# Rotary embedding without a swapped copy of its input, and half a chunk of weights made later

## The chip, the cores and the metric

One core of a Trainium2 chip runs the whole program. The metric is the device time of one execution in microseconds (us). Engines: TensorE (PE) multiplies matrices, with its weight loads shown apart as PEld; VectorE (DVE) and ScalarE (ACT) do elementwise work; GpSimd (POOL) does nothing here but set a tile to one; SyncE (SP) issues the DMAs.

## What is computed

Two transformer blocks on 256 tokens of 1024 features, float32. The first has a mixer with two kinds of attention, MLA (8 heads, 64 plain and 32 rotated query and key features) and a forgetting attention ("fox"), and a gated feed-forward with a convolution over three tokens. The second has two layers (differential attention, then MOBA), each with a squared-ReLU feed-forward. What the change touches is the rotation:

```
def rope(x, positions):
    ...
    x1, x2 = xf[..., : r // 2], xf[..., r // 2:]
    out = jnp.concatenate([x1 * cos - x2 * sin, x2 * cos + x1 * sin], axis=-1)

q = ((q_lat normed) @ w_uq).reshape(b, s, MLA_HEADS, 96)   # 64 plain, 32 to be rotated
k_mla = concatenate([k_nope, broadcast(k_rope, 8 heads)])
scores = q_mla . k_mla * MLA_SCALE                          # contracted over 96 features
```

## The kernel before, in words

**Weights.** All weights but the adaptive ones (ada) are read once, in chunks of 128 partitions by 2048 columns (`weight_order`, chunk n is `ORDER[n]`). A chunk goes by DMA into one of four raw buffers, then in two halves of 1024 columns into whi (rounded to the short float32 form; ScalarE, line 1545, for three chunks VectorE, line 1941) and wlo (the remainder, VectorE, line 1949). TensorE forms each product in three matmuls, whi by high part, whi by low part, wlo by high part (lines 1070 to 1072). whi and wlo have three slots, four from chunk ("out", 0) on. The step `weights` of chunk n + 3 (or n + 4) is put where chunk n is done, by `refill(n)`, and waits for chunk n's last matmul in the slot that it takes. `refill` also takes one of the waiting small jobs (`chores`).

**Order.** `stages()` writes one list of steps; each engine's program walks through the list and issues its own part of every step. So an engine's queue has the order of the list, and an instruction waits behind all that stands ahead of it.

**The rotary part.** ("uq", 0) holds the 512 plain query features, ("uq", 1) the 512 others: for each of 8 heads the 32 rotary features, and again the same 32 with their halves swapped. Each is three weight tiles deep (384 latent features), 1536 columns used. ("uq", 1) runs in two pairs of banks, `pr` 0 (rotary) and 1 (swapped): 2 x 2 x 3 x 3 = 36 matmuls. In step `ev_uq_rope` VectorE multiplies the first by COS and the second by SIN (line 2219), whose sign was set per partition by the step `signs` (line 2055), and adds both, 512 columns (line 2223). In `copy_rope` ScalarE copies the result in four instructions to rows 64 to 96 of QM (line 1719). The key's 32 rotary features are treated alike: `turn_key` (lines 2208 to 2211) on a copy and a swapped copy, and `copy_key` (line 1713) spreads them to 8 heads in KM. The scores of MLA contract rows 0 to 96 of QM and KM (lines 1469 and 1470).

Steps around it, in order: tokens ("in", 7) with the scores of fox head pair 0; both pairs of ("uq", 1) in banks 0 and 1; tokens ("in", 8) in bank 2; rows of ("ukv", 0) in banks 3 and 0, copied out by ScalarE (lines 1690, 1691); its values in banks 1 and 2 (lines 1319 to 1321); then the gate chunks ("in", 9) in bank 0, ("in", 10) in bank 1, and on, each with one step of attention between its halves: values of one head pair (1503, 1504), transposes of the next (`turn`, line 1481, of the probabilities that VectorE scales in line 2286), scores of the one after (1469, 1470). After ("in", 16) come the output products, whose gates VectorE applies (line 2230).

**The end of the first feed-forward.** `down(9)` is followed by `refill`, which puts there the first half of the weights of ("qkv0", 1). Then `last_down`: the last 24 matmuls of the down product (lines 1362 to 1364) are split so that the output features 0 to 511 are done first. ScalarE evicts them (`delta`, line 1883), TensorE transposes them (`delta_turned`, line 1399), VectorE updates the residual X, one pair of tiles at a time (`ev_down`, line 2335), and ScalarE and VectorE make from it the next input HX, high (line 1660) and low part (`gain`), ScalarE its square (line 1587):

```
emit("delta_turned", kind, 0)
take(0)                     # ev_down 0, gain 0
rest(0)                     # square 0
emit("down_tokens", n, kind, i, pairs, LAST_BY_OUTPUTS[6:8])
emit("delta", n, kind, 1, 0)
take(1)                     # ev_down 1, gain 1
emit("delta", n, kind, 1, 1)
rest(1)
if kind == "down":
    other_half(st["halves"])
```

`other_half` makes the second half of ("qkv0", 1) and issues the next DMA. The products of ("qkv0", 0) and ("qkv0", 4) follow (lines 1223 to 1226); after their second input tile the other features are transposed, and pairs 2 and 3 updated. Then come the sums of squares (line 1080).

Of the kernel before, what the change touches and what calls it, by code (L numbers as in the profile page):

```python
# [12 lines left out]
ACT = mybir.ActivationFunctionType  # L13

T = 256
# [23 lines left out]
def _columns():  # L39
    at = 0  # L40
    for name, n in [
        ("c", 8), ("b_ada", 48), ("norm_mix_g", 8), ("norm_ffn_g", 8), ("norm_final_g", 8),
        ("q_norm_g", 3), ("kv_norm_g", 2), ("conv_w", 132), ("conv_b", 44), ("attn_norm", 16),
        ("mlp_norm", 16), ("subln", 1), ("b_forget", 1), ("invf", 1), ("sgn", 1),
        ("eps", 1), ("m1", 8), ("m2", 8), ("m3", 1), ("m4", 1), ("id", 128),
    ]:
        COLS[name] = at
        at += n
    return at
# [28 lines left out]
USED = {"uq": 1536}  # L78
# [51 lines left out]
def stages():  # L130
# [210 lines left out]
    for i in range(7):  # L341
# [71 lines left out]
    rows(("uq", 1), "lat", pairs=2, mid=False, evac=ev_uq_rope)  # L413
# [133 lines left out]
    def last_down(kind, i, pairs, take, rest):  # L547
# [9 lines left out]
        rest(0)  # L557
        emit("down_tokens", n, kind, i, pairs, LAST_BY_OUTPUTS[6:8])
# [281 lines left out]
def _build(nc, ctx, wall, wada, smalls, pos, xt, masks, lam4, alibi8, alibi16, gfin, out):  # L840
# [130 lines left out]
    def hi_mark(n):  # L971

        return "v_whi" if n in BOTH_PARTS else "a_whi"
# [5 lines left out]
    def half_cols(n, half):  # L979
        return slice(half * CH // 2, min(USED.get(ORDER[n][0], CH), (half + 1) * CH // 2))  # L980

# [4 lines left out]
    def sync(e):  # L986
# [4 lines left out]
        def load(i):  # L991
# [9 lines left out]
            else:  # L1001
                n = USED.get(it[2], CH)
# [45 lines left out]
    def tensor(e):  # L1048
# [7 lines left out]
        def weights_there(n, last):  # L1056
# [5 lines left out]
            on.wait_ge(hi_mark(n), (n, (last - 1) // (CH // 2)))  # L1062
            on.wait_ge("v_wlo", (n, (last - 1) // (CH // 2)))
# [44 lines left out]
        for step, *a in STEPS:  # L1108
# [121 lines left out]
            elif step == "rows":  # L1230
                n, src, b, pr, nt = a
                hi, lo, kts, ncols, x0 = features(n, src)
                slot = place(n)
# [182 lines left out]
            elif step == "ev_uq_rope":  # L1416
                free[a[1]] = ("v_qr", a[2])
# [107 lines left out]
    def scalar(e):  # L1525
# [9 lines left out]
        for step, *a in STEPS:  # L1535
# [175 lines left out]
            elif step == "copy_key":  # L1711
                on.wait_ge("v_kr", "turned")
                e.activation(
                    KM[64:96, :, :], V[64:96, 0, 256:512].unsqueeze(1).to_broadcast([32, 8, T]), ACT.Copy).then_inc(
                    *up("a_kr", 0))
# [194 lines left out]
    def vector(e):  # L1910
# [18 lines left out]
        def trig_there():  # L1929
            on.wait_ge("a_sin", 0)  # L1930
            on.wait_ge("v_rope", "signs")

        for step, *a in STEPS:
# [119 lines left out]
            elif step == "signs":  # L2053
                on.wait_ge("a_sin", 1)
                e.tensor_scalar(SIN[:, :], SIN[:, :], col("sgn"), None, ALU.mult).then_inc(*up("v_rope", "signs"))
# [148 lines left out]
            elif step == "turn_key":  # L2204
                k0, k1 = V[64:96, 0, 256:512], V[64:96, 1, 256:512]
                on.wait_ge("a_ev", (FIRST, 1))
                trig_there()
                e.tensor_tensor(k0, FK[64:96, :], COS[64:96, :], ALU.mult)
                e.tensor_tensor(k1, FK[96:128, :], SIN[96:128, :], ALU.mult).then_inc(*up("v_kr", "parts"))
                on.wait_ge("v_kr", "parts")  # L2210
                e.tensor_tensor(k0, k0, k1, ALU.add).then_inc(*up("v_kr", "turned"))
            elif step == "ev_uq_rope":
                n, b, pr = a
                dst, table = ((TT[:, :, :], COS), (SQ[:, 0:2, :], SIN))[pr]
                on.wait_ge("t_mm", (n, pr))
# [3 lines left out]
                e.tensor_tensor(dst, two(b), table[:, :].unsqueeze(1).to_broadcast([128, 2, T]), ALU.mult).then_inc(  # L2219
                    *up("v_qr", pr))  # L2220
                if pr == 1:
                    on.wait_ge("v_qr", 1)
                    e.tensor_tensor(TT[:, :, :], TT[:, :, :], SQ[:, 0:2, :], ALU.add).then_inc(*up("v_qr", "sum"))
                    tt_free[0] = tt_free[1] = ("a_qr", 0)
# [241 lines left out]
def _chunks(a):  # L2466
# [4 lines left out]
    sw = np.concatenate([r(16, 32), r(16)])  # L2471
    cols_in = np.concatenate([cq, np.tile(ff, 8), kr, kr[sw], ckv, fk, fq, fv, gm, gf])
    uq = np.concatenate([p + 96 * h for p in (r(64), 64 + r(32), 64 + sw) for h in range(8)])
# [4 lines left out]
    for kind, i in weight_order():  # L2478
# [5 lines left out]
        elif kind == "uq":  # L2484
            t = np.pad(_tiles(a["w_uq"][0], uq[512 * i:512 * i + 512]), ((0, 0), (0, 512)))
# [29 lines left out]
def _smalls(a):  # L2515
    def tiles(v):
# [12 lines left out]
        one(lambda q: -1.0 if q % 32 < 16 else 1.0), one(lambda q: EPS), m1, m2,  # L2529
# [40 lines left out]
```

## Time and profile before

| | |
|---|---|
| median of 3 runs | 1001.15 us (1000.82 to 1001.93) |
| profiled execution, its own time | 1001.78 us |
| its span in the profile | 999.7 us |
| busy: PE / PEld / DVE / ACT | 990.8 / 892.3 / 719.3 / 596.9 us |
| granted TensorE clock | 1.00 of full speed throughout |
| DMA | 196.73 MB, mean 197 GB/s |
| chain that ended last | PE 79%, DVE 13%, ACT 6% |

A row of the timeline gives the start and the duration in us, the engine, the line of the kernel, what is written and read, the number of instructions merged into the row, and in brackets the idle time before it and whom it waited for. Instructions of one engine overlap, so the distance between two starts is shorter than the duration.

### The profile page before, as it was taken

How to read it: one execution, taken by the hardware profiler on the slowest of the kernel's cores; microseconds unless marked ns; L12 is line 12 of the kernel's file. 1: busy time of each engine (PE TensorE's matmuls, PEld its weight loads, DVE VectorE, ACT ScalarE, POOL GpSimd, SP SyncE). 2: the span in 40 equal slices, each digit the busy share in tenths (PEclk: the TensorE clock that was granted, in tenths of full speed). 3: DMA queues.
4: the chain of work that ended last, by engine and by line, in shares of the span. 5: the costliest groups of instructions: out<-in, count | busy, mean ns of one | idle time of the engine just before them, and what ended most of it. 6: DMA issues, size and time to landing. Idle time of an engine off the chain costs nothing.

```text
span 999.7 us, 16660 instructions
## 1 busy us (share of the span) xinstructions
PE 990.8 (99%) x6652; PEld 892.3 (89%) x6652; DVE 719.3 (72%) x1225; ACT 596.9 (60%) x1010; POOL 0.4 (0%) x5
## 2 busy tenths in 40 slices
PE   9999999999999999999999999999999999999997
PEld 8899999998888888899999888888999899888886
DVE  5898888878888888887658665655776558565652
ACT  4778666557566657767647445554665547455452
POOL 0000000000000000000000000000000000000000
PEclk9999999999999999999999999999999999999999
DMA  9975668535656564563326655556554337555521
GB/s 367 396 248 178 267 231 297 202 138 211 210 197 231 222 238 168 209 211 127 127 85 218 207 207 200 180 179 206 213 189 142 127 106 253 193 186 174 207 83 43
DMA packets 28444, 196.73 MB, mean 197 GB/s; under 512 B 3152, under 2 KB 3664, under 8 KB 5584
## 3 DMA queue, kind: packets, MB, share of 16 engines
q1 hardware_dynamic: 28224, 195.41, 55.1%
q8 instruction: 54, 0.88, 0.4%
q10 hardware_dynamic: 144, 0.26, 0.1%
q14 instruction: 22, 0.18, 0.1%
HBM read 194.61 MB, written 1.05 MB: 196 GB/s over the span
## 4 chain that ended last, share of the span: by engine, by line
PE 79%; DVE 13%; ACT 6%; issue 2%; POOLq 0%; DVEq 0%; ACTq 0%
PE PS L1383 16%; PE PS L1270 10%; PE PS L1070 8%; PE PS L1071 7%; PE PS L1072 7%; DVE wlo L1949 7%; PE PS L1274 5%; PE PS L1223 3%; PE PS L1226 3%; PE PS L1224 3%; ACT whi L1545 2%; ACT PB L1833 2%; PE PS L1304 2%; PE PS L1305 2%; PE PS L1306 2%
## 5 line engine op out<-in xcount | busy, mean ns | idle before, releaser
L1949 DVE TENSOR_TENSOR wlo<-raw,whi 128x1024 fp32r<-128x1024 f32 x306 | 358.4, 1217 | 60.4 <-ACT whi L1545 57.8
L1545 ACT ACTIVATE whi<-raw 128x1024 fp32r<-128x1024 f32 x300 | 297.8, 1046 | 58.7 <-PE PS L1383 53.2
L1270 PE MATMUL PS<-HX,whi 128*128 128x512 f32 x736 | 231.1, 395 | 0.0
L1274 PEld LDWEIGHTS PS<-HX,wlo 128*128 128x128 f32 x736 | 138.3, 188 | 32.3
L1070 PE MATMUL PS<-HX,whi 128*128 128x256 f32 x496 | 145.2, 293 | 0.6 <-DVE HX L1923 0.6
L1274 PE MATMUL PS<-HX,wlo 128*128 128x256 f32 x736 | 144.7, 278 | 0.0
L1071 PE MATMUL PS<-HX,whi 128*128 128x256 f32 x496 | 140.3, 283 | 0.0
L1072 PE MATMUL PS<-HX,wlo 128*128 128x256 f32 x496 | 140.2, 283 | 0.0
L1270 PEld LDWEIGHTS PS<-HX,whi 128*128 128x128 f32 x736 | 114.5, 189 | 2.6
L1070 PEld LDWEIGHTS PS<-HX,whi 128*128 128x128 f32 x496 | 94.9, 191 | 5.9 <-issue 4.3
L1071 PEld LDWEIGHTS PS<-HX,whi 128*128 128x128 f32 x496 | 95.0, 192 | 0.2
L1072 PEld LDWEIGHTS PS<-HX,wlo 128*128 128x128 f32 x496 | 94.9, 191 | 0.0
L1383 PE MATMUL PS<-whi,Oh 128*128 128x512 f32 x240 | 74.3, 391 | 0.0
L1383 PE MATMUL PS<-wlo,Oh 128*128 128x512 f32 x240 | 73.9, 389 | 0.0
L1383 PE MATMUL PS<-whi,Ol 128*128 128x512 f32 x240 | 73.9, 389 | 0.0
L1853 ACT ACTIVATE PB<-PS 128x512 f32<-128x512 f32 x26 | 15.5, 598 | 84.1 <-PE PS L1274 84.1
L2434 DVE TENSOR_TENSOR PB<-PS,PB 128x512 f32<-128x512 f32 x26 | 18.0, 692 | 64.0 <-ACT PB L1853 64.0
L1223 PE MATMUL PS<-HX,whi 128*128 128x256 f32 x192 | 54.8, 285 | 0.9 <-ACT HX L1660 0.7
L1226 PE MATMUL PS<-HX,whi 128*128 128x256 f32 x192 | 54.7, 285 | 0.0
L1224 PE MATMUL PS<-HX,wlo 128*128 128x256 f32 x192 | 54.3, 283 | 0.0
L1383 PEld LDWEIGHTS PS<-wlo,Oh 128*128 128x128 f32 x240 | 45.1, 188 | 9.6
L1383 PEld LDWEIGHTS PS<-whi,Ol 128*128 128x128 f32 x240 | 45.1, 188 | 9.4
(276 smaller groups left out, 1820.5 us busy)
## 6 DMA issues: line engine op xcount, KB each, us to landing
raw<-wall SPq DMA_DIRECT2D x151, 1024.0 KB, 5.1
raw<-wada SPq DMA_DIRECT2D x18, 1024.0 KB, 5.1
raw<-wall SPq DMA_DIRECT2D x8, 512.0 KB, 16.2
GA<-wada SPq DMA_DIRECT2D x2, 1024.0 KB, 20.2
GA<-alibi SPq DMA_DIRECT2D x1, 2048.0 KB, 9.7
raw<-wall SPq DMA_DIRECT2D x2, 768.0 KB, 5.8
X<-xt SPq DMA_DIRECT2D x1, 1024.0 KB, 5.0
KM<-wada SPq DMA_DIRECT2D x1, 1024.0 KB, 14.2
```

Of the source, the lines that this page charges most:

```text
L1070: e.matmul(dst, wh, a, start=start, stop=False, skip_group_check=share)
L1071: e.matmul(dst, wh, b, start=False, stop=False, skip_group_check=share)
L1072: return e.matmul(dst, wl, a, start=False, stop=stop, skip_group_check=share)
L1223: e.matmul(dst, wh, hi[:, k, :], start=k == 0 and nt == 0, stop=False, skip_group_check=True)
L1224: e.matmul(dst, wl, hi[:, k, :], start=False, stop=False, skip_group_check=True)
L1226: m = e.matmul(dst, wh, lo[:, k, :], start=False, stop=k == 7, skip_group_check=True)
L1270: e.matmul(PS[:, b + nt, :], whi[place(n)][:, at + nt * 128:at + nt * 128 + 128], HX[:, k, :, :].rearrange("p h t -> p (h t)"), start=k == ...
L1274: m = e.matmul(PS[:, b + nt, 0:T], wlo[place(n)][:, at + nt * 128:at + nt * 128 + 128], Hh[:, k, :], start=False, stop=k == 7, skip_group_ ...
L1304: e.matmul(dst, hi, whi[slot][:, c], start=k == 0, stop=False)
L1383: m = e.matmul(PS[:, 4 + 2 * t + c, :], x, w[:, at:at + 512], start=first and part == 0, stop=False, skip_group_check=True)
L1545: e.activation(whi[place(n)][:, c], raw[i % RAW][:, c], ACT.Copy).then_inc(*up("a_whi", (n, half)))
L1949: e.tensor_tensor(wlo[place(n)][:, c], raw[i % RAW][:, c], f32(whi[place(n)][:, c]), ALU.subtract).then_inc(*up("v_wlo", (n, half)))
```

## The change

**Rotary.** ("uq", 1) holds only the 256 rotary features of 8 heads, ordered so that bank half 0 has the first halves (16 features of each head) and bank half 1 the second. It is 768 columns, made in two parts of 512 and 256, and takes 18 matmuls in one bank; the bank counter is moved on by one more, so that all later steps have the banks they had. VectorE forms the products of both halves with COS and with SIN (two instructions of 512 columns), then a difference and a sum of 256 columns each. Each 32 rows of the result hold two heads. ScalarE copies the first halves to rows 64 to 96 of QM, to both heads; a new step `copy_second` has VectorE copy the second halves, in four instructions of 32 x 512, to rows 96 to 128, after the weights of ("in", 10). KM gets, by two instructions with a mask per partition (`even`, `odd`), the key's features only in the rows of the head in question and zero in the others, and the scores contract all 128 rows. The step `signs` goes; `turn_key` takes four instructions instead of three, on 64 rows where it had 32.

**Half chunk.** The `refill` behind `down(9)` moves into `last_down`, behind `rest(0)`.

```
-USED = {"uq": 1536}
+USED = {("uq", 0): 1536, ("uq", 1): 768}
+HALF = {("uq", 1): 512}
...
-            emit("signs")
...
     def ev_uq_rope(n, b, pr):
-        emit("ev_uq_rope", n, b, pr)
-        if pr == 1:
-            chores.append(lambda: emit("copy_rope"))
+        emit("ev_uq_rope", n, b)
+        chores.extend([lambda: emit("copy_rope"), lambda: emit("copy_second")])
...
-    rows(("uq", 1), "lat", pairs=2, mid=False, evac=ev_uq_rope)
+    rows(("uq", 1), "lat", mid=False, evac=ev_uq_rope)
+    st["at"] += 1
...
             emit("down_tokens", n, "down", i, 11, DOWN_PARTS)
             st["done"] = n
-            if i == 9:
-                st["halves"] = NUMBER[("qkv0", QKV_ORDER[2])]
-            refill(n)
+            if i < 9:
+                refill(n)
...
         take(0)
         rest(0)
+        if kind == "down":
+            st["halves"] = NUMBER[("qkv0", QKV_ORDER[2])]
+            refill(NUMBER[("down", 9)])
         emit("down_tokens", n, kind, i, pairs, LAST_BY_OUTPUTS[6:8])
...
-                        q, k = QM[0:96, h, :], KM[0:96, h, :]
+                        q, k = QM[:, h, :], KM[:, h, :]
+                        on.wait_ge("v_qr", "copied")
...
-                    KM[64:96, :, :], V[64:96, 0, 256:512].unsqueeze(1).to_broadcast([32, 8, T]), ACT.Copy)
+                for h0, mask in ((0, "even"), (1, "odd")):
+                    m = e.activation(
+                        KM[64:128, h0:8:2, :], V[64:128, 0, 256:512].unsqueeze(1).to_broadcast([64, 4, T]), ACT.Identity,
+                        scale=col(mask, 0, 1, 64, 128))
...
-                    m = e.activation(QM[64:96, j:8:4, :], TT[32 * j:32 * j + 32, :, :], ACT.Copy)
+                        QM[64:96, 2 * j:2 * j + 2, :], TT[32 * j:32 * j + 32, 0, :].unsqueeze(1).to_broadcast([32, 2, T]), ACT.Copy)
...
+                e.tensor_tensor(k0, FK[64:128, :], COS[64:128, :], ALU.mult)
+                e.scalar_tensor_tensor(k1[64:96], FK[96:128, :], -1.0, SIN[96:128, :], ALU.mult, ALU.mult)
+                e.tensor_tensor(k1[96:128], FK[64:96, :], SIN[64:96, :], ALU.mult)
+                e.tensor_tensor(k0, k0, k1[64:128], ALU.add)
...
+                e.tensor_tensor(TT[:, :, :], two(b), cosines, ALU.mult)
+                e.tensor_tensor(SQ[:, 0:2, :], two(b), sines, ALU.mult).then_inc(*up("v_qr", "parts"))
+                on.wait_ge("v_qr", "parts")
+                e.tensor_tensor(TT[:, 0, :], TT[:, 0, :], SQ[:, 1, :], ALU.subtract)
+                e.tensor_tensor(TT[:, 1, :], TT[:, 1, :], SQ[:, 0, :], ALU.add).then_inc(*up("v_qr", "sum"))
+            elif step == "copy_second":
+                on.wait_ge("v_qr", "sum")
+                for j in range(4):
+                    m = e.tensor_copy(
+                        QM[96:128, 2 * j:2 * j + 2, :], TT[32 * j:32 * j + 32, 1, :].unsqueeze(1).to_broadcast([32, 2, T]))
+                m.then_inc(*up("v_qr", "copied"))
```

## Rows read from the trace of the kernel before

**Rows 1.** The page, part 1: busy time, share, instructions of each engine.

```profile
PE 990.8 (99%) x6652; PEld 892.3 (89%) x6652; DVE 719.3 (72%) x1225; ACT 596.9 (60%) x1010; POOL 0.4 (0%) x5
```

**Rows 2.** All waits of PE, 54 to 399 us: total, times, longest.

```profile
PE PS L1223 <- ACT HX L1652: 0.2, 1, 0.2
```

**Rows 3.** Timeline of PE: first matmul of ("uq", 1), and the step after it.

```profile
79.34 0.29 PE L1070 MATMUL PS<-Oh,whi 128*128 128x256 f32 x1
...
83.66 0.28 PE L1304 MATMUL PS<-whi,HX 128*128 128x256 f32 x1
```

**Rows 4.** Timeline of DVE: the sign step.

```profile
44.35 0.35 DVE L2055 TENSOR_SCALAR SIN<-SIN,SM 128x256 f32<-128x256 f32 x1
```

**Rows 5.** DVE by line and form, 50 to 105 us: busy us, mean ns, idle before.

```profile
L1949 DVE TENSOR_TENSOR wlo<-raw,whi 128x1024 fp32r<-128x1024 f32 x18 | 21.3, 1217 | 1.1 <-ACT whi L1545 1.0
...
L1941 DVE CAST whi<-raw 128x1024 fp32r<-128x1024 f32 x4 | 2.7, 686 | 0.0
...
L2118 DVE SCALAR_TENSOR_TENSOR TT<-PB,SM,RB 128x256 f32<-128x256 f32 x5 | 2.2, 482 | 0.2
...
L2203 DVE COPY QM<-PS 64x512 f32<-64x512 f32 x2 | 1.4, 693 | 0.0
...
L1949 DVE TENSOR_TENSOR wlo<-raw,whi 128x512 fp32r<-128x512 f32 x2 | 1.4, 678 | 0.0
...
L1941 DVE CAST whi<-raw 128x512 fp32r<-128x512 f32 x2 | 0.8, 414 | 0.0
```

**Rows 6.** Timeline of DVE: the sum of both products.

```profile
87.88 0.69 DVE L2223 TENSOR_TENSOR TT<-TT,SQ 128x512 f32<-128x512 f32 x1
```

**Rows 7.** Timeline of ACT: the copy of the queries, and the instruction that frees bank 0.

```profile
88.60 2.56 ACT L1719 ACTIVATE QM<-TT 32x512 f32<-32x512 f32 x4 [1.51 <-DVE TT L2223]
...
96.14 0.60 ACT L1691 ACTIVATE KM<-PS 64x512 f32<-64x512 f32 x1
```

**Rows 8.** Timeline of PE: first matmul of ("in", 9); transposes of mla head pair 2.

```profile
97.02 0.28 PE L1070 MATMUL PS<-HX,whi 128*128 128x256 f32 x1
...
145.14 0.87 PE L1481 MATMUL PS<-SM,PB 128*128 128x128 f32 x6
```

**Rows 9.** Timeline of DVE: scaled probabilities of that pair; two waits for ACT.

```profile
142.47 1.01 DVE L2286 TENSOR_SCALAR PB<-PB,RS 128x128 f32<-128x128 f32 x4
...
166.79 2.36 DVE L1949 TENSOR_TENSOR wlo<-raw,whi 128x1024 fp32r<-128x1024 f32 x2 [0.67 <-ACT whi L1545]
170.27 0.69 DVE L2230 TENSOR_TENSOR GA<-PS,GA 128x512 f32<-128x512 f32 x1 [1.12 <-ACT GA L1789]
```

**Rows 10.** Timeline of PE at the end of the first feed-forward.

```profile
400.28 0.98 PE L1399 MATMUL PS<-SM,ACC 128*128 128x128 f32 x7 [0.16 <-ACT ACC L1883]
...
403.34 0.36 PE L1223 MATMUL PS<-HX,whi 128*128 128x256 f32 x1 [0.69 <-ACT HX L1660]
...
406.51 1.04 PE L1399 MATMUL PS<-SM,ACC 128*128 128x128 f32 x8
...
417.80 0.66 PE L1080 MATMUL PS<-ONES,PB 128*128 128x64 f32 x4 [0.66 <-DVE PB L2162]
```

**Rows 11.** Timeline of DVE there: updates of X, and the second half chunk.

```profile
402.18 0.87 DVE L2335 SCALAR_TENSOR_TENSOR X<-PS,ADA,X 128x256 f32<-128x256 f32 x2
...
404.03 0.87 DVE L2335 SCALAR_TENSOR_TENSOR X<-PS,ADA,X 128x256 f32<-128x256 f32 x2
...
408.23 1.23 DVE L1949 TENSOR_TENSOR wlo<-raw,whi 128x1024 fp32r<-128x1024 f32 x1 [1.05 <-ACT whi L1545]
409.38 0.87 DVE L2335 SCALAR_TENSOR_TENSOR X<-PS,ADA,X 128x256 f32<-128x256 f32 x2
```

**Rows 12.** Timeline of ACT there: square, eviction, second half chunk.

```profile
403.50 0.62 ACT L1587 ACTIVATE SQ<-X 128x512 f32<-128x512 f32 x1
...
405.36 0.57 ACT L1883 ACTIVATE ACC<-PS 128x512 f32<-128x512 f32 x1
...
407.16 1.04 ACT L1545 ACTIVATE whi<-raw 128x1024 fp32r<-128x1024 f32 x1
```

More of the change, by code:

```diff
@@ L979, in half_cols, with half_with @@
     def half_cols(n, half):
-        return slice(half * CH // 2, min(USED.get(ORDER[n][0], CH), (half + 1) * CH // 2))
+        cut = HALF.get(ORDER[n], CH // 2)
+        return slice(half * cut, min(USED.get(ORDER[n], CH), (half + 1) * cut))
+    def half_with(n, last):
+        return (last - 1) // HALF.get(ORDER[n], CH // 2)
     STEPS = stages()
@@ L1061, in weights_there @@
                 return
-            on.wait_ge(hi_mark(n), (n, (last - 1) // (CH // 2)))
-            on.wait_ge("v_wlo", (n, (last - 1) // (CH // 2)))
+            on.wait_ge(hi_mark(n), (n, half_with(n, last)))
+            on.wait_ge("v_wlo", (n, half_with(n, last)))
         def split_there(key):
@@ L1232, in tensor @@
                 hi, lo, kts, ncols, x0 = features(n, src)
+                if ORDER[n] == ("uq", 1):
+                    ncols = 256
                 slot = place(n)
@@ L1416, in tensor @@
             elif step == "ev_uq_rope":
-                free[a[1]] = ("v_qr", a[2])
+                free[a[1]] = ("v_qr", "parts")
             elif step == "gated":
@@ L2204, in vector @@
             elif step == "turn_key":
-                k0, k1 = V[64:96, 0, 256:512], V[64:96, 1, 256:512]
+                k0, k1 = V[64:128, 0, 256:512], V[:, 1, 256:512]
                 on.wait_ge("a_ev", (FIRST, 1))
                 trig_there()
-                e.tensor_tensor(k0, FK[64:96, :], COS[64:96, :], ALU.mult)
-                e.tensor_tensor(k1, FK[96:128, :], SIN[96:128, :], ALU.mult).then_inc(*up("v_kr", "parts"))
+                e.tensor_tensor(k0, FK[64:128, :], COS[64:128, :], ALU.mult)
+                e.scalar_tensor_tensor(k1[64:96], FK[96:128, :], -1.0, SIN[96:128, :], ALU.mult, ALU.mult)
+                e.tensor_tensor(k1[96:128], FK[64:96, :], SIN[64:96, :], ALU.mult).then_inc(*up("v_kr", "parts"))
                 on.wait_ge("v_kr", "parts")
-                e.tensor_tensor(k0, k0, k1, ALU.add).then_inc(*up("v_kr", "turned"))
+                e.tensor_tensor(k0, k0, k1[64:128], ALU.add).then_inc(*up("v_kr", "turned"))
             elif step == "ev_uq_rope":
-                n, b, pr = a
-                dst, table = ((TT[:, :, :], COS), (SQ[:, 0:2, :], SIN))[pr]
-                on.wait_ge("t_mm", (n, pr))
+                n, b = a
+                on.wait_ge("t_mm", (n, 0))
                 trig_there()
@@ L2218, in vector @@
                 on.wait_ge("t_sq", "kv")
[L2219 to L2224, printed above, removed]
+                cosines, sines = (x[:, :].unsqueeze(1).to_broadcast([128, 2, T]) for x in (COS, SIN))
+                e.tensor_tensor(TT[:, :, :], two(b), cosines, ALU.mult)
[3 more added lines that the diff above has]
+                e.tensor_tensor(TT[:, 1, :], TT[:, 1, :], SQ[:, 0, :], ALU.add).then_inc(*up("v_qr", "sum"))
+                tt_free[0] = tt_free[1] = ("a_qr", 0)
+            elif step == "copy_second":
[4 more added lines that the diff above has]
+                m.then_inc(*up("v_qr", "copied"))
             elif step == "gated":
@@ L2470, in _chunks @@
     cq, ckv, kr, fq, fk, fv, ff, gm, gf = (r(cut[i], cut[i + 1]) for i in range(9))
-    sw = np.concatenate([r(16, 32), r(16)])
-    cols_in = np.concatenate([cq, np.tile(ff, 8), kr, kr[sw], ckv, fk, fq, fv, gm, gf])
-    uq = np.concatenate([p + 96 * h for p in (r(64), 64 + r(32), 64 + sw) for h in range(8)])
+    kr1, kr2 = kr[0:16], kr[16:32]
+    cols_in = np.concatenate([cq, np.tile(ff, 8), kr1, kr1, kr2, kr2, ckv, fk, fq, fv, gm, gf])
+    uq = np.concatenate([p + 96 * h for p in (r(64), 64 + r(16), 80 + r(16)) for h in range(8)])
     ukv = np.concatenate([np.concatenate([r(64) + 128 * h for h in range(8)]),
@@ L2484, in _chunks @@
         elif kind == "uq":
[L2485 removed]
+            t = _tiles(a["w_uq"][0], uq[512 * i:512 * i + 512])
+            t = np.pad(t, ((0, 0), (0, 2048 - t.shape[1])))
         elif kind == "ukv":
@@ L2528, in _smalls @@
         np.tile(a["b_forget"][0], 16)[:, None], inv[p % 16][:, None].astype(np.float32),
-        one(lambda q: -1.0 if q % 32 < 16 else 1.0), one(lambda q: EPS), m1, m2,
+        one(lambda q: 1.0 if q % 32 < 16 else 0.0), one(lambda q: 0.0 if q % 32 < 16 else 1.0), one(lambda q: EPS), m1, m2,
         one(lambda q: -8.0 if q >= 8 else 0.0), one(lambda q: 1.0 if q < 8 else 0.0),
```

15 lines of the change are left out of this document (5 added, 10 removed).

## The prediction

> **What bounds the kernel now.** I read the busy shares first. TensorE (PE) is busy for 990.8 of 999.7 us [rows 1]. The other engines have idle time, so shortening their work pays only where TensorE waits for them. The waits of TensorE come next: between 54 and 399 us, the stretch with the mixer, there is one wait, of 0.2 us [rows 2]. The timeline of TensorE says the same more finely: its 256-column matmuls start every 0.12 us, whatever duration the row gives, so work is costed here by distance between starts. A matmul left out is worth 0.12 us if, and only if, everything that TensorE asks for next is ready that much earlier. So the second thing to read is how far ahead ScalarE (ACT) and VectorE (DVE) are. The margins turn out small, and they decide the case.
>
> The place of the second edit is where TensorE does wait: 0.69 us at 403.34 and 0.66 us at 417.80 [rows 10]. Both waits end in work that VectorE had queued, so that stretch is set by VectorE, not by TensorE.
>
> **Part 1, the rotary edit: what TensorE is spared.** The 36 matmuls of ("uq", 1) run from 79.34 to 83.66, when the next step begins [rows 3]: 4.32 us, 0.12 each. 18 remain, so 2.16 us of TensorE's work go. The MLA scores contract over 128 rows instead of 96; the program has the fox scores on 80 rows and the MLA scores on 96 in one pattern of starts, so I take no cost.
>
> **What ScalarE and VectorE can follow.** VectorE's queue runs almost without a gap from the sign step to the query products, so I add up its changes.
> - The sign step goes: 0.35 us busy [rows 4], about 0.26 between starts.
> - turn_key has one more instruction, a scalar_tensor_tensor on 256 columns: +0.48 [rows 5].
> - Both weight parts of ("uq", 1) are made on VectorE, and now 768 columns instead of 1536. By the rows of 1024 and 512 columns, 512 columns are worth 0.686 - 0.414 = 0.27 us in the cast and 1.217 - 0.678 = 0.54 in the subtraction [rows 5]; 768 columns are 1.5 times 0.81: -1.22.
> Together -1.0 us where the products for the queries begin. There the two products stay and the one sum of 512 columns (0.69) [rows 6] becomes two of 256, about 0.34 to the second start and 0.42 more, so +0.07. The rotated queries are thus there 0.9 us earlier. The key copy on ScalarE becomes two instructions of half the length on twice the partitions, at most 0.1 us more, and there is about that much room before the first exponentials.
>
> ScalarE starts to copy the queries at 88.60, the moment the sum is there [rows 7], and from that copy to the instruction at 96.14 it has no gap; that one, ending at 96.74, frees bank 0. TensorE starts the rows of ("in", 9) in bank 0 at 97.02 [rows 8], close behind. With a handover of some 0.1 us there is 0.2 us of room. So TensorE, 2.16 us early until then, is stopped here: it can be ahead by 0.9 + 0.2 = **1.1 us** only. "The bank count kept" makes this the same bank as before.
>
> Next come VectorE's four new copies (copy_second), 32 x 512 each, SBUF to SBUF, for the second halves of the queries. No such copy is in the trace. The lower bound is the cast of 512 columns, 0.41 us; the upper one is the copy of 512 columns out of PSUM, 0.69 [rows 5]. I take 0.42, as the cast too has one source and lies in SBUF; the range keeps 1.7 to 2.8 us for all four. VectorE was 0.9 early and is then 0.8 late (up to 1.9). Nobody waits for the copies themselves until the MLA scores, two chunks later, but all the work queued behind them shifts. The tightest handover that I find is the transposes for mla head 2: VectorE finishes the scaled probabilities at 142.47 + 1.01 = 143.48 [rows 9], and TensorE transposes from 145.14, its fifth, the first that needs the last product, some 0.48 later [rows 8]. That is 2.14 us of room, and 1.1 + 0.8 = 1.9 uses it up nearly. With slow copies TensorE would keep 2.14 - 1.9 = 0.3 us of its lead. VectorE loses its lateness at 166.79 and 170.27, where it sat waiting 0.67 and 1.12 us for ScalarE [rows 9], which in turn had been waiting for TensorE. After that the three engines run together, 1.1 us early.
>
> The Trainium skill (VectorE: DVE Perf Modes, "What auto-detection actually checks") says that a one-source instruction goes at double rate only when source and destination both lie in SBUF with suitable outer dimensions; no row here has these very copies. By it all four would take the low price and the sum below would stand; at the upper price the lead would be 0.3 us and the sum 1001.9.
>
> The DMA of ("uq", 1) falls from 768 to 384 KB. No engine waits for a landing in this stretch, so it is costed at nothing; its cover is the four raw buffers. No DMA issue moves, neither SP's nor POOL's, since a half chunk issues none before its second half.
>
> **Part 2, the half chunk.** The step is the first half of ("qkv0", 1): a copy to whi on ScalarE, then a subtraction to wlo on VectorE, which waits for that copy. Before, they stood ahead of the last down product. Now they stand after the square of the first output pair.
> - *Gain.* VectorE has five wlo in a row in its queue, 1.22 us each [rows 5] and 1.15 from start to start, and behind them the residual update at 402.18 [rows 11]. With four it comes 1.15 us earlier, at 401.03. ScalarE's evictions come earlier too, so the transposes lose their 0.16 us gap [rows 10]. TensorE resumes at 402.19 instead of 403.34.
> - *Loss.* ScalarE starts that square at 403.50 [rows 12], now 402.35. Its next start is 0.53 later: whi from 402.88 to 403.92. VectorE has been done with pair 0 since 402.88 (404.03 less 1.15) and sits 1 us waiting, since the wlo is next in its queue. It runs from 403.95, and the update of pair 1, queued behind it, starts at 405.10, where it was at 404.03 [rows 11]: **1.07 us late**. ScalarE's gain of pair 1 waits for that, and the eviction behind it goes from 405.36 [rows 12] to 406.43. The eight transposes of TensorE that began at 406.51 [rows 10] need it complete, at about 407.05, though TensorE is at their place at 405.36, again 1.15 earlier. The second half of the chunk follows: its whi moves from 407.16 to 408.23 [rows 12], its wlo from 408.23 to 409.30, the update of pair 2 from 409.38 to 410.45 [rows 11]. From there to the sum of squares at 417.80 [rows 10], for which TensorE waits, the chain has no gap to give it back: 418.87.
> So part 2 gains 1.15 us and then gives back all and 1.07 more. The queue's order, not the amount of work, does this.
>
> **The sum.** -1.1 + 1.07 = -0.03. The profiled run took 1001.78 (span 999.7 and 2.1 around it), 0.63 over the median of 1001.15. From the profiled run: 1001.75; less 0.63: **1001.1 us**. A measurement of this kernel can tell about 0.2%, 2.0 us, from no change.
>
> **Rivals.**
> - *Both edits pay in full.* TensorE keeps 2.16 us, and the moved step leaves the 1.15: 1001.15 - 3.3 = 997.8. For it: 99% busy, and a real cut of work. Against: the bank at 97.02 with 0.2 us of room, and the wlo queued ahead of the update. A variant: only the handover after 403 is kinder than I read it, -1.1 - 1.15: 998.9. Chance 0.14 together, half for each.
> - *The rotary edit keeps 2.16 us, the half chunk costs 1.07*: 1000.1. It needs the rotated queries 2 us early. Chance 0.15, counted as no change.
> - *VectorE becomes the bound between 100 and 165 us (slower).* The four copies delay each scaled probability; above 2.14 us of lead and lateness together TensorE pays. At 0.69 each: 1001.15 - 0.3 + 1.07 = 1001.9. From 3.0 us for the four on, nothing of the lead is left, and at 4 us, 1 each, the sum is +2.1: 1003.2. Against: no 512-column row of one source is above 0.69. Chance 0.13, of which 0.07 past 0.2%.
> - *My forecast* has the rest, 0.58.
>
> **Numbers.** Faster by over 0.2%: 0.14. Slower: 0.07. Within: 0.79. The bounds of the costs alone give 1000.1 to 1001.9; the range reaches down to the variant at 998.9 and leaves out the full payment (0.07) and the end of the third rival (0.07); with some scatter of the measurement it is 998.8 to 1002.4.
>
> **What would show it.** Right: 18 matmuls for ("uq", 1); a start of ("in", 9) near 95.9, right behind ScalarE's copy, with a gap of TensorE before it of 1 us; VectorE waiting about 1 us for whi between the updates of pairs 0 and 1; TensorE with a gap of over 1 us before its second set of transposes. Wrong: ("in", 9) starting near 94.9; copies above 0.7 us; the update of pair 1 no later, against TensorE's own pace, than before.

## The result, and the profile after

The changed kernel takes 1003.64 us (median of 16 runs, 1002.90 to 1004.28), the kernel before 1001.31 us (16 runs, 1000.82 to 1001.97). The ratio is 1.0022, 95% interval 1.0015 to 1.0028: slower by 2.3 us. The median is outside the forecast range, and over the 0.2% mark, on the side that had a chance of 0.07; the interval holds 1.0020 too, so that the loss is real is sure, and that it is over 0.2% is not. The profiled execution took 1002.96 us, its span is 1001.0.

The page of the changed kernel, part 1, answers to [rows 1]:

```profile
PE 988.3 (99%) x6634; PEld 888.9 (89%) x6634; DVE 720.1 (72%) x1230; ACT 596.9 (60%) x1011; POOL 0.4 (0%) x5
```

The 18 matmuls are gone and TensorE is 2.5 us less busy, while the span is 1.3 us longer. So the time is in waits. All waits of TensorE between 54 and 402 us in the changed kernel (engine and line that waits, releaser, total, times, longest), where [rows 2] had one of 0.2 us up to 399:

```profile
PE PS L1077 <- ACT GA L1749: 1.7, 1, 1.7
PE PS L1077 <- ACT KM L1701: 0.7, 1, 0.7
PE PS L1328 <- ACT V L1738: 0.2, 1, 0.2
```

The second is the one that was forecast, bank 0 at ("in", 9). The third stands 2.3 us ahead of it and also waits for ScalarE to free a bank. The first, the largest, was not forecast.

**Where the time went.** TensorE runs almost without a gap, so the distance between two of its landmarks is a good clock. I use three: the first matmul of ("uq", 1), the first transpose of the last down product (`delta_turned`), and the sum of squares after the first residual updates. Before they stood at 79.34 [rows 3], 399.81 and 417.80 [rows 10]; here is the second, and then all three of the changed kernel, from the timelines of PE:

```profile
399.81 0.31 PE L1399 MATMUL PS<-SM,ACC 128*128 128x128 f32 x1
```

```profile
78.37 0.29 PE L1077 MATMUL PS<-Oh,whi 128*128 128x256 f32 x1
...
399.98 1.03 PE L1408 MATMUL PS<-SM,ACC 128*128 128x128 f32 x8
...
419.05 0.66 PE L1087 MATMUL PS<-ONES,PB 128*128 128x64 f32 x4 [0.66 <-DVE PB L2171]
```

| stretch | before | after | difference |
|---|---|---|---|
| up to ("uq", 1), untouched by the change | 79.34 | 78.37 | -0.97 |
| ("uq", 1) to the transposes: the rotary edit | 320.47 | 321.61 | +1.14 |
| transposes to the sum of squares: the half chunk | 17.99 | 19.07 | +1.08 |
| sum of squares to the end of the span | 581.90 | 581.95 | +0.05 |

The first line is no effect of the change. It differs between profiles of every kernel here, from -0.97 to +0.21 (table below). The other three add up to 2.27 us, and the medians differ by 2.33. Times "net" below are differences to the kernel before, at the same instruction, after removing the 0.97 (or the lead-in of the run in question).

**The rotary stretch.** VectorE first. Each fence has rows of one timeline of the changed kernel, here DVE: first scores of fox head pair 0, the second of the two new sums, the new copies, and the low part of the attention output with which its next step begins.

```profile
78.12 0.29 DVE L2276 CUSTOM_DVE_ANT_0 PB<-PS,TRI 128x128 f32<-128x128 f32 x1
...
86.61 0.42 DVE L2233 TENSOR_TENSOR TT<-TT,SQ 128x256 f32<-128x256 f32 x1
...
99.18 1.72 DVE L2238 COPY QM<-TT 32x512 f32<-32x512 f32 x4
...
103.22 0.42 DVE L1936 TENSOR_TENSOR Ol<-PS,Oh 128x256 fp32r<-128x256 f32 x1
```

Two rows of the kernel before that answer to the first and the last of these:

```profile
80.14 0.29 DVE L2260 CUSTOM_DVE_ANT_0 PB<-PS,TRI 128x128 f32<-128x128 f32 x1
...
103.00 0.42 DVE L1923 TENSOR_TENSOR Ol<-PS,Oh 128x256 fp32r<-128x256 f32 x1
```

VectorE is 1.05 us early (net) at 78.12, and 1.19 us late (net) at 103.22. ScalarE, in the changed kernel: the key copy, the table load, the first exponentials, the query copy, the instruction that frees bank 0, then the last exponentials of fox head 3 and the eviction behind them.

```profile
75.69 2.19 ACT L1724 ACTIVATE KM<-V,SM 64x1024 f32<-64x1024 f32 x2
77.90 1.28 ACT L1756 ACT_TABLE_LOAD   x1
79.19 0.40 ACT L1756 ACTIVATE PB<-PB,NM 128x128 f32<-128x128 f32 x1
...
87.06 2.55 ACT L1731 ACTIVATE QM<-TT 32x512 f32<-32x512 f32 x4 [1.59 <-DVE TT L2233]
...
94.59 0.59 ACT L1701 ACTIVATE KM<-PS 64x512 f32<-64x512 f32 x1
...
113.04 0.40 ACT L1756 ACTIVATE PB<-PB,NM 128x128 f32<-128x128 f32 x1 [3.57 <-DVE NM L2279]
...
114.81 0.57 ACT L1749 ACTIVATE GA<-PS 128x512 f32<-128x512 f32 x1
```

And TensorE: ("in", 9), then ("in", 11).

```profile
95.24 0.39 PE L1077 MATMUL PS<-HX,whi 128*128 128x256 f32 x1 [0.65 <-ACT KM L1701]
...
115.44 0.39 PE L1077 MATMUL PS<-HX,whi 128*128 128x256 f32 x1 [1.71 <-ACT GA L1749]
```

The reader should follow the last one back. The rows of ("in", 11) go to bank 1. The same bank held ("in", 10), because two transposed sums of the adaptive weights (`ada_sum`) take banks 2 and 0 between them. ScalarE frees bank 1 with the eviction at 114.81, behind four exponentials, the first of which waited 3.57 us for VectorE's scores. So VectorE's lateness goes through ScalarE to TensorE in one chain. The rows of the kernel before at this place, ACT's eviction and TensorE's start:

```profile
114.60 0.57 ACT L1736 ACTIVATE GA<-PS 128x512 f32<-128x512 f32 x1
```

```profile
114.37 1.04 PE L1194 MATMUL PS<-SM,ACC 128*128 128x128 f32 x8
115.23 0.38 PE L1070 MATMUL PS<-HX,whi 128*128 128x256 f32 x1
```

The eviction ended at 114.60 + 0.57 = 115.17 and TensorE went on at 115.23. In the changed kernel it ended at 114.81 + 0.57 = 115.38, and TensorE, which did wait for it, went on at 115.44. The distance is 0.06 us both times, so this is what the handover itself takes, and the kernel before had no room here at all. It was even held up a little: from the first transpose to the first matmul of ("in", 11) it took 115.23 - 114.37 = 0.86 us, and 0.79 in e12 below, where the bank is another one. The list of waits shows nothing at this place.

**The half chunk.** DVE in the changed kernel (answers to [rows 11]), and PE (answers to [rows 10]):

```profile
401.21 0.87 DVE L2351 SCALAR_TENSOR_TENSOR X<-PS,ADA,X 128x256 f32<-128x256 f32 x2
...
404.14 1.22 DVE L1961 TENSOR_TENSOR wlo<-raw,whi 128x1024 fp32r<-128x1024 f32 x1 [0.99 <-ACT whi L1555]
405.28 0.87 DVE L2351 SCALAR_TENSOR_TENSOR X<-PS,ADA,X 128x256 f32<-128x256 f32 x2
```

```profile
405.54 0.27 PE L1408 MATMUL PS<-SM,ACC 128*128 128x128 f32 x1
407.24 0.98 PE L1408 MATMUL PS<-SM,ACC 128*128 128x128 f32 x7 [1.43 <-ACT ACC L1896]
```

VectorE waits 0.99 us for whi, the update of pair 1 stands behind it, and TensorE has a gap of 1.43 us in its second set of transposes. ScalarE is not what is late there: before its gain of pair 1, at 405.79, it sits idle for 1.21 us, waiting for that update.

### The profile page after: what moved, and what is told of

Same layout as the page of the kernel before. It is cut to its first block, busy times and chain, and to the rows that moved or that the text cites. A ratio compares the mean times of both kernels' runs of the same rounds, so it can differ in the third digit from the quotient of the medians.

```text
span 1001.0 us, 16630 instructions
## 1 busy us (share of the span) xinstructions
PE 988.3 (99%) x6634; PEld 888.9 (89%) x6634; DVE 720.1 (72%) x1230; ACT 596.9 (60%) x1011; POOL 0.4 (0%) x5
## 3 DMA queue, kind: packets, MB, share of 16 engines
HBM read 194.21 MB, written 1.05 MB: 195 GB/s over the span
## 4 chain that ended last, share of the span: by engine, by line
PE 70%; DVE 16%; ACT 9%; issue 3%; DMA 2%; POOLq 0%; DVEq 0%; ACTq 0%
PE PS L1392 16%; PE PS L1279 10%; DVE wlo L1961 8%; PE PS L1077 6%; PE PS L1078 6%; PE PS L1079 6%; PE PS L1283 5%; ACT whi L1555 3%; PE PS L1230 3%; PE PS L1233 3%; PE PS L1231 3%; ACT PB L1846 2%; DVE PB L2425 2%; DMA raw<-wall 2%; PE PS L1313 2%
## 5 line engine op out<-in xcount | busy, mean ns | idle before, releaser
L1961 DVE TENSOR_TENSOR wlo<-raw,whi 128x1024 fp32r<-128x1024 f32 (+1 forms) x306 | 357.6, 1214 | 61.4 <-ACT whi L1555 58.7
```

The source lines that it names most:

```text
L1961: e.tensor_tensor(wlo[place(n)][:, c], raw[i % RAW][:, c], f32(whi[place(n)][:, c]), ALU.subtract).then_inc(*up("v_wlo", (n, half)))
```

## The experiments

All were timed beside the kernel before, 11 runs each (e3 has 5). "R" below is the change's rotary edit alone, with the half chunk where the kernel before has it. The table has, for every kernel, the difference of its median to that of the kernel before timed beside it, the ratio with its interval, and, from its own timeline of PE, the stretches of the table above as differences to the profile of before. The half-chunk stretch repeats to 0.1 us. The rotary stretch repeats to 0.2: e1 has in it what the change has, and shows +1.33 beside +1.14. The medians differ from the sum of the stretches by up to 0.4.

| kernel | median less before | ratio, 95% | lead-in | rotary stretch | half-chunk stretch |
|---|---|---|---|---|---|
| the change | +2.33 | 1.0022 [1.0015, 1.0028] | -0.97 | +1.14 | +1.08 |
| e1 R alone | +1.31 | 1.0010 [1.0001, 1.0019] | -0.38 | +1.33 | +0.02 |
| e2 half chunk alone | +1.41 | 1.0012 [1.0003, 1.0021] | -0.68 | -0.01 | +1.04 |
| e3 R, banks moved on by one | +3.74 | 1.0039 [1.0026, 1.0051] | -0.71 | +3.84 | 0.00 |
| e4 half chunk, whi at the old place | +0.25 | 1.0001 [0.9992, 1.0010] | -0.23 | -0.01 | +0.01 |
| e5 R, copies in VectorE's gaps | -0.88 | 0.9994 [0.9985, 1.0003] | +0.21 | -0.64 | 0.00 |
| e9 R, ada sums in banks 6 and 7 | +0.47 | 1.0005 [0.9996, 1.0013] | -0.23 | +0.76 | 0.00 |
| e10 R, e5 and e9 together | -0.94 | 0.9990 [0.9982, 0.9999] | -0.33 | -0.64 | 0.00 |
| e11 as e10, ScalarE's copies later | -0.85 | 0.9995 [0.9986, 1.0004] | -0.22 | -0.43 | +0.01 |
| e12 before, ada sums in 6 and 7 | -0.38 | 0.9996 [0.9988, 1.0005] | -0.28 | -0.06 | +0.02 |
| e15 half chunk, both whi early | -1.10 | 0.9988 [0.9979, 0.9997] | -0.57 | +0.03 | -1.12 |
| e16 e10 and e15 together | -1.88 | 0.9981 [0.9972, 0.9990] | -0.02 | -0.62 | -1.11 |
| e17 the change, copies in the gaps | +0.39 | 1.0005 [0.9997, 1.0014] | -0.52 | -0.56 | +1.11 |

**Which edit costs what (e1, e2).** e1 is the change with this part taken back, e2 the kernel before with this part alone:

```
-            if i == 9:
-                st["halves"] = NUMBER[("qkv0", QKV_ORDER[2])]
-            refill(n)
+            if i < 9:
+                refill(n)
...
         rest(0)
+        if kind == "down":
+            st["halves"] = NUMBER[("qkv0", QKV_ORDER[2])]
+            refill(NUMBER[("down", 9)])
```

> The rotary edit alone, the half chunk at its old place. Theory A (VectorE's four new copies make ScalarE's eviction of ("in", 10) late, and the rows of ("in", 11) wait for it in the same bank): +1.2 us against before, with one wait of TensorE of 1.7 us at 115. Theory B (the step of the forecast: the lead is kept after ("in", 9)): -1.1 us. Theory C (the half chunk alone makes the change slower): 0.

> The half chunk alone, on the kernel before. Theory A and B: +1.1 us, with a wait of TensorE of 1.4 us before its second set of transposes. Theory C: +2.3 us.

Each costs over 1 us, in its own stretch and nowhere else, and they add up: 1.33 + 1.04 = 2.37, beside 1.14 + 1.08 = 2.22 in the change's own stretches and 2.33 between its medians.

**More room by another bank, first attempt (e3).** R with one line more, ahead of the rows of the gate chunks:

```
     for g in range(8):
+        st["at"] += g == 2
         rows(("in", 9 + g)
```

> The rotary edit alone, and the bank counter moved on by one before ("in", 11), so that it does not take the bank of ("in", 10). Theory A: the wait at 115 goes, TensorE keeps the lead of 0.8 us that it has from ("in", 9) on: -0.8 us. Rival D (VectorE's lateness meets TensorE anyway, at the next handover): the wait moves on and the time stays at +1.2 us.

Neither theory had it: +3.74. ("in", 11) now takes bank 2, in which the first ada sum lies. The timeline of PE in e3:

```profile
112.94 1.03 PE L1201 MATMUL PS<-SM,ACC 128*128 128x128 f32 x8
117.06 0.58 PE L1077 MATMUL PS<-HX,whi 128*128 128x256 f32 x1 [3.08 <-DVE ADA L2015]
117.44 0.42 PE L1078 MATMUL PS<-HX,whi 128*128 128x256 f32 x1
117.65 0.41 PE L1079 MATMUL PS<-HX,wlo 128*128 128x256 f32 x1
```

It waits 3.08 us for VectorE's reduction of that sum, which is queued behind the scaling of the probabilities, where in R it waited 1.7. Afterwards the matmuls start 0.21 us apart instead of 0.12. The windows of e3 (length, busy us and count of PE, PEld, DVE, ACT, POOL, then granted clock, DMA share, GB/s) say why:

```profile
114.00:117.00 3.00, 0.00 (x0) 0.00 (x0) 1.78 (x6) 3.00 (x9) 0.00 (x0) 0.96 0.91 352
117.00:120.20 3.20, 3.14 (x15) 3.15 (x16) 3.10 (x7) 0.53 (x1) 0.00 (x0) 0.51 0.06 20
```

The granted clock is 0.51 for the 3.2 us after the idle time, the lower level, 1.2 GHz. Some 14 matmuls at 0.09 us more make another 1.3 us. The change's wait of 1.7 us had no such sequel: its matmuls go on 0.12 us apart.

**What in the half chunk costs (e4).** The kernel before with only VectorE's part of the half chunk moved, ScalarE's copy left at the old place:

```
-                    emit("weights", i, it[1], (0,))
+                    emit("weights_hi", i, it[1], (0,))
...
         rest(0)
+        if kind == "down":
+            emit("weights_lo", ITEM_OF[st["halves"]], st["halves"], (0,))
```

> The kernel before, with the half chunk split: its copy to whi on ScalarE at the old place, its subtraction to wlo on VectorE at the new one. Theory A (the loss is VectorE's wait for whi, 1.0 us): 0 us against before. Rival E (the subtraction ahead of the update of pair 1 costs, whoever is waited for): +1.1 us.

The loss is gone: +0.01 in the stretch. What cost 1.07 us was VectorE's wait for whi, which comes from ScalarE's copy at the new place. The subtraction takes, ahead of the update of pair 1, only the 1.15 us that its leaving gave to the update of pair 0, so it costs nothing on balance.

**The copies or the bank (e9, e5, e10).** e9 is R with another place for the ada sums, e5 is R with another place for the copies, e10 both.

```
         for half in range(2):
-            emit("ada_sum", cb, half, 4 + half if cb == 3 or "late" in st else bank())
+            emit("ada_sum", cb, half, 6 + half if cb == 2 else 4 + half if cb == 3 or "late" in st else bank())
```

```
-        chores.extend([lambda: emit("copy_rope"), lambda: emit("copy_second")])
+        chores.append(lambda: emit("copy_rope"))
...
+    def ev_gate(n, b, g):
+        emit("ev_gate", n, b, g)
+        if g < 2:
+            emit("copy_second", g)
...
-                for j in range(4):
+                for j in range(2 * a[0], 2 * a[0] + 2):
```

> The rotary edit alone, with the two late sums of the ada part 2 put in banks 6 and 7 instead of 2 and 0, so that the rows of ("in", 11) take bank 2 and not bank 1 behind ("in", 10). Theory A (TensorE loses its lead at the one handover of bank 1, to which VectorE's lateness comes by way of ScalarE's exponentials): the wait of 1.7 us ahead of ("in", 11) is gone, VectorE's 1.2 us of lateness stays inside the room of 2.14 us at the transposes of mla head 2, and TensorE keeps its 0.8 us: 1001.3 - 0.8 = 1000.5. Rival B (VectorE sets the pace wherever TensorE meets it, the bank is only the first place): the wait turns up at a later handover before 145 us, and the time stays at 1002.5. Rival D (as in the run that shifted the banks by one, the new place waits for VectorE's reduction of the ada sums): 1003 or more.

> The rotary edit alone, with VectorE's four new copies issued two and two behind the evictions of ("in", 9) and ("in", 10), where VectorE waits for the exponentials, instead of all four ahead of them. Banks as in the change. Theory A (the cost of the rotary edit is the four copies in VectorE's queue ahead of scores that ScalarE, and then bank 1, wait for): VectorE is no longer late at 103 us, the wait ahead of ("in", 11) shrinks from 1.7 to at most 0.3 us, and TensorE keeps 0.6 us: 1000.7. Rival C (the copies have nothing to do with it; the slower key copy or the bank of ("in", 9) is what costs): 1002.6, as without this edit. Rival E (the gaps are too narrow, and the copies delay the same scores from there): between, 1001.5.

> Both of the two edits before together: the rotary edit with its copies in VectorE's gaps, and the late ada sums in banks 6 and 7. Theory A: no wait at ("in", 11) at all, and TensorE keeps what it has ahead at ("in", 9), 0.8 us: 1000.5, no more than either edit alone, since both remove the same wait. Rival B (each of them hides a different delay): 1.2 us and more below the single edits.

In e9 the wait at ("in", 11) is gone, and another has come, in the timeline of PE:

```profile
150.46 1.12 PE L1200 MATMUL PS<-SM,ACC 128*128 128x128 f32 x8 [1.14 <-DVE NM L2278]
```

This is the next ada sum, in banks 4 and 5, which VectorE frees when it has done the scores of two mla heads. Here is the instruction that frees bank 4, in the kernel before and in e9, and between them TensorE's transposes of the kernel before:

```profile
149.06 0.09 DVE L2263 DVE_READ_ACCUMULATOR2_ANT NM<- 128x1 f32 x1
```

```profile
150.05 1.04 PE L1194 MATMUL PS<-SM,ACC 128*128 128x128 f32 x8
```

```profile
150.23 0.08 DVE L2278 DVE_READ_ACCUMULATOR2_ANT NM<- 128x1 f32 x1
```

VectorE is still as late as it was at 103 us: it frees the bank at 150.31, before at 149.15, so 1.16 later, or 1.39 net of the lead-in. In e9 TensorE starts 0.15 us after that, so the room in the kernel before was 150.05 - 149.15 - 0.15 = 0.75 us. VectorE's 1.39 and the 0.58 us by which TensorE was ahead, less 0.75, make 1.22, and TensorE goes from 0.58 ahead to 0.64 behind there. So my theory A had the right mechanism and the wrong extent: over half of R's loss came back at the next handover, +0.76 in the stretch where A had -0.8. Rival B, VectorE as the pace-maker wherever TensorE meets it, was nearer.

In e5 the lateness itself is taken away. The timeline of DVE in e5:

```profile
102.61 0.42 DVE L1941 TENSOR_TENSOR Ol<-PS,Oh 128x256 fp32r<-128x256 f32 x1
...
104.16 0.85 DVE L2243 COPY QM<-TT 32x512 f32<-32x512 f32 x2
105.50 0.18 DVE L2291 RECIPROCAL RS<-RS 128x4 f32<-128x4 f32 x1 [0.49 <-ACT PB L1764]
```

The same instruction that came at 103.22 in the change (1.19 us late, net) comes at 102.61, 0.60 early net of e5's own lead-in. The two copies lie in a wait for the exponentials that was 1.4 us long and of which 0.49 remains. TensorE keeps 0.64 us of its lead to the end of the stretch. With both edits (e10) it is again 0.64, but that this is the same number is partly chance. Behind ("in", 9) e5 has 0.72 us of lead and e10 0.49, which no edit of theirs explains; at ("in", 11), e5, in the old bank, loses 0.11 of it, and e10 gains 0.07. So with the lateness gone the bank is worth 0.2 us at most.

**The next limit (e11).** As e10, with ScalarE's copies of the queries moved from ahead of the exponentials of fox head 1 to ahead of those of fox head 2:

```
+        if scored == 2 and heads.pop("rope", False):
+            emit("copy_rope")
```

> As the run before, and ScalarE's four copies of the rotated queries are moved behind the evictions of ("in", 7) and ("in", 8), into its idle time ahead of the exponentials of fox head 2. Theory A (the handover of bank 0 at ("in", 9) is what cuts TensorE's lead from 2.16 to 0.8 us, because those copies stand ahead of the eviction that frees it): ("in", 9) starts nearly 2 us earlier than before and the whole stretch follows: 1001.3 - 2.0 = 999.3, less what the next handover takes; 999.3 to 1000.0. Rival C (ScalarE would have been late by its exponentials anyway): 1000.5, as the run before.

Neither theory had all of it: ("in", 9) starts 1.25 us early (net) instead of 0.6, but the gain is lost again, and the stretch ends at -0.43 against -0.64 in e10. ScalarE in e11:

```profile
90.84 0.40 ACT L1763 ACTIVATE PB<-PB,NM 128x128 f32<-128x128 f32 x1 [3.65 <-DVE NM L2286]
...
101.45 2.55 ACT L1738 ACTIVATE QM<-TT 32x512 f32<-32x512 f32 x4
104.02 0.40 ACT L1763 ACTIVATE PB<-PB,NM 128x128 f32<-128x128 f32 x1
```

Two things are seen. With the copies out of its way ScalarE sits 3.65 us waiting for VectorE's scores, so it is VectorE that cuts the lead at ("in", 9). And at 101.45 the copies need more time than the idle time that they were to fill: the exponentials behind them start at 104.02, at once, where e10 had them at 103.30. VectorE then runs late, and TensorE waits 0.6 us for it at 149.33, at the ada sum of e9. The room found there fits again: TensorE is 1.22 us ahead and VectorE 0.25 late, less 0.75 is 0.72, and TensorE's lead goes from 1.22 to 0.50.

**Control (e12).** The bank edit of e9 on the kernel before.

> Control: the kernel before, with nothing but the late ada sums in banks 6 and 7. Theory A (the handover of bank 1 at ("in", 11) has 0.06 us of room in the kernel before but nobody waits there, so more room is worth nothing): 0, within 0.2 us of before. Rival H (the banks by themselves gain, and part of what the runs with both edits showed was theirs): -0.3 or more.

Its stretch is -0.06, and the interval of its ratio holds 1. The median is lower by 0.38, which rival H would want, but the stretches do not show it, and medians scatter by about as much. The 0.06 can be found in the rows of ACT and PE at ("in", 11) of e12:

```profile
114.33 0.57 ACT L1736 ACTIVATE GA<-PS 128x512 f32<-128x512 f32 x1
```

```profile
114.09 1.03 PE L1194 MATMUL PS<-SM,ACC 128*128 128x128 f32 x8
114.88 0.36 PE L1070 MATMUL PS<-HX,whi 128*128 128x256 f32 x1
```

TensorE starts before ScalarE's eviction is over (114.90), and 0.79 us after the first transpose, where the kernel before took 0.86. So theory A is wrong in one word: TensorE did wait for bank 1 in the kernel before, by 0.07 us, and that is all that the bank edit gains by itself.

**The half chunk taken apart properly (e15).** The move of e4, and ScalarE's copy of the second half taken ahead too, behind the evictions of the first deltas:

```
         for t in range(2):
             emit("delta", n, kind, 0, t)
+        if kind == "down":
+            emit("weights_hi", ITEM_OF[st["halves"]], st["halves"], (1,))
...
     def other_half(n):
-        emit("weights", i, n, (1,))
+        emit("weights_lo", i, n, (1,))
```

> The kernel before with the half chunk of ("qkv0", 1) taken apart in another way: VectorE's subtraction for the first half at the change's place, but ScalarE's copies for neither half there: that of the first half stays at its old place, and that of the second half moves forward to behind the evictions of the first deltas, where ScalarE sits idle for 2.5 us. Theory A (what counts is that VectorE never waits for a copy to whi; it waits 1.05 us for the second half's in the kernel before already): the first residual update comes 1.15 us earlier, that of pair 1 no later, and that of pair 2 1.1 us earlier than before, and TensorE's wait at the sum of squares goes: 1001.4 - 1.1 = 1000.3. Rival F (TensorE's own 13 us of matmuls in that stretch are the bound, VectorE's waits are hidden): 0 to -0.3, 1001.2. Rival G (ScalarE is late by the copy put ahead of the gain): +0.5.

It gains 1.12 us in the stretch. DVE in e15:

```profile
405.97 0.69 DVE L2079 TENSOR_TENSOR SQ<-SQ 128x512 f32<-128x512 f32 x1 [0.51 <-ACT SQ L1591]
406.58 1.22 DVE L1953 TENSOR_TENSOR wlo<-raw,whi 128x1024 fp32r<-128x1024 f32 x1
407.71 0.87 DVE L2339 SCALAR_TENSOR_TENSOR X<-PS,ADA,X 128x256 f32<-128x256 f32 x2
```

The subtraction of the second half follows its predecessor at once. In the kernel before it waited 1.05 us for whi [rows 11], a wait that was there to be had all along. One part of theory A was wrong: TensorE's wait of 0.66 us at the sum of squares stays (0.65 in e15). The sum is simply asked for and ready 1.12 us earlier.

**Both together (e16), and the change with one line moved (e17).** e16 is e10 with the half chunk of e15. e17 is the whole change with the copies of e5 and nothing else.

> The rotary edit with VectorE's new copies in its gaps and the late ada sums in banks 6 and 7, and with the half chunk taken apart as in the run before. Theory A: the two stretches are 230 us apart and TensorE is busy between them, so their gains add: -0.9 and -1.1 against the kernel before, 999.4. Rival: a common limit further on (final sums, DMA) takes one of them: 1000.5.

> The whole change, with VectorE's four new copies issued two and two in its waits for the exponentials and nothing else: the half chunk is where the change puts it. Theory A: -0.9 for the rotary edit and +1.1 to +1.4 for the half chunk against the kernel before: 1001.4 + 0.3 = 1001.7, 2 us less than the change as it stands. Rival C (the order of the copies only matters without the half chunk): 1003.6.

e16 takes 999.61 us (median of 11 runs) beside 1001.49 of the kernel before, 0.9981 [0.9972, 0.9990]. It is faster than both kernels; its stretches are -0.62 and -1.11, the sum of the two causes. e17 takes 1001.88: moving the four copies takes 1.9 us off the change as it stands by the medians and 1.7 by the stretches, and what is left is the half chunk's 1.1 less the rotary edit's 0.6.

## Why the prediction was wrong, point by point

- *Part 1, TensorE spared 2.16 us.* Right: the step behind ("uq", 1) starts at 80.53 beside 83.66, 2.16 ahead net. Nothing shows a cost of the contraction over 128 rows: TensorE is 1.18 behind at ("in", 11) and 1.14 at the transposes near 400, with all MLA scores between.
- *VectorE 1.0 us ahead before the products.* Right up to the scores of fox head pair 0, 1.05 net; at the products it is 0.64 (84.95 beside 86.56). The queue is not "almost without a gap": between these two VectorE waits 1.38 us for ScalarE's exponentials in the kernel before, and 1.78 in the changed one.
- *The rotated queries 0.9 us earlier.* 0.57. A smaller error: "at most 0.1 us more, and there is about that much room" for the key copy. It began 0.14 later net (75.69 beside 76.52), and two instructions of half the length took 2.19 us instead of 1.92. The table load stands behind them, and the first exponentials started right behind that, 0.65 early instead of 1.0.
- *The lead limited by bank 0 at ("in", 9) to 1.1 us.* The place is right. The size is 0.81, less by the same 0.3 (0.59 in e1). e11 adds that behind ScalarE's copies VectorE's scores were the next limit.
- *Four copies at 0.42 us each.* Right: 1.72 for four. The Trainium skill (VectorE: DVE Perf Modes, "What auto-detection actually checks") says that the double rate wants source and destination in SBUF; this trace agrees, with 0.43 us for 32 x 512 beside 0.69 for the same count out of PSUM [rows 5].
- *VectorE then 0.8 late.* 1.19, again the 0.3 to 0.4 above.
- **The step that failed:** "The tightest handover that I find is the transposes for mla head 2", with 2.14 us of room. The tightest was bank 1 at ("in", 11), 30 us earlier, with no room at all; the second, the ada sum at 150.05 in banks 4 and 5, with 0.75. I looked at transfers of data (who reads the scaled probabilities) and took only ("in", 9) of the transfers of banks. Both that I missed are of the second kind, and both stand where an ada sum comes between. So no lead was kept, and 1.14 us were lost instead of 1.1 gained: an error of 2.2 us in one term, nearly the whole miss of 1003.64 - 1001.31 + 0.03 = 2.4. My third rival had the right engine (VectorE between 100 and 165 us), but at its own place, with the room of 2.14, so that the four copies had to take over 3 us before the rotary edit cost anything; they took 1.7.
- *Part 2, the half chunk: +1.07.* Right, in size and mechanism: +1.08 in the change, +1.04 alone. The forecast times of the updates also hold, once the lead-in and part 1's loss (0.17 together at the transposes) are added: pair 0 at 401.03, seen 401.21; pair 1 at 405.10, seen 405.28; the sum of squares at 418.87, seen 419.05. e4 shows that the wait for whi is the cause.
- *Chances.* Two steps of some 1 us each, of opposite sign, were forecast to cancel. With one handover missed they add. The range took in the bounds of the costs, but not a handover that I had not seen, and the lateness of 0.8 us that I had computed made such a handover likely to matter.

What stays open: why the same rotary edit shows +1.14 in one profile and +1.33 in another, and what sets the moment at which TensorE's clock rises at the start (last section), on which most of the lead-in hangs.

## What to carry to other kernels

When a change makes an engine late, do not look for the waits that exist; go through every handover to the busy engine behind that point, banks and buffers as well as data, and write down the room of each, because the one that decides may be missing from the list of waits (here it had no room at all and was not in it). The time from the release to the start is not yet room: find what the handover itself takes, 0.06 us here, at a place where the engine did wait. Put added work where its engine already waits for something that does not depend on it: moving the same four copies in the queue was worth 1.7 to 1.9 us. And when a two-engine step is moved, move only the half that was in the way; the other engine's half should stand early, in that engine's own idle time.

## What the runs showed of the hardware

**The lead-in.** Both kernels begin with the same 56 warm-up matmuls (`PE L1121`, which are L1114 before). The first sum behind them begins at 8.83 us in the changed kernel and at 9.86 in the kernel before, which accounts for the -0.97 of the table.

```profile
8.83 1.90 PE L1087 MATMUL PS<-ONES,SQ 128*128 128x64 f32 x16
```

```profile
9.86 1.90 PE L1080 MATMUL PS<-ONES,SQ 128*128 128x64 f32 x16
```

Windows of both, the changed kernel first (the first count is that of TensorE's matmuls):

```profile
4.00:6.00 2.00, 2.00 (x19) 2.00 (x19) 0.00 (x0) 0.98 (x2) 0.00 (x0) 1.00 0.99 414
6.00:8.00 2.00, 2.00 (x20) 2.00 (x20) 1.75 (x3) 1.15 (x2) 0.00 (x0) 1.00 0.99 416
```

```profile
4.00:6.00 2.00, 2.00 (x11) 2.00 (x11) 0.00 (x0) 1.10 (x2) 0.00 (x0) 1.00 0.99 410
6.00:8.00 2.00, 2.00 (x19) 2.00 (x18) 1.76 (x3) 1.15 (x2) 0.00 (x0) 1.00 0.99 416
```

The warm-up matmuls start 0.21 us apart at first and 0.11 apart later, and the pace turns at 4.1 us in the changed kernel and at 6.3 in the kernel before. The trace's own record of the granted clock begins at just these moments (4.14 and 6.30 us, at full speed); the windows have no record before it and print 1.00. Over all fourteen profiles that record begins between 3.89 us (e2, first sum at 8.71) and 6.68 us (e16, first sum at 10.04), in no order that follows the edits. Waits further on add to it: e5 has its first sum at 9.00, but is 0.21 us later than the kernel before at ("uq", 1), with waits of 0.7 us for ScalarE and 0.5 for a transfer on the way.

**The clock after a wait.** In e3, 3.08 us without a matmul brought the granted clock to the 1.2 GHz level for the next 3.2 us, while the change's 1.71 us left it at 1.00.
